# Output projection of the recurrence block with tokens on partitions, last slab by token halves, result scaled and turned by products with a diagonal

## The reference

```python
mix_out = jnp.einsum("bsd,de->bse", merged, w_out[layer])
x = x + rms_norm_2(mix_out, mix_norm_post[layer])
h = rms_norm_2(x, ffn_norm_pre[layer])
up = jnp.einsum("bsd,df->bsf", h, w_up[layer])
up = causal_dwconv(up, conv_f_w[layer], conv_f_b[layer])
gate, val = jnp.split(up, 2, axis=-1)
ffn_out = jnp.einsum("bsf,fd->bsd", jax.nn.gelu(gate) * val, w_down[layer])
x = x + rms_norm_2(ffn_out, ffn_norm_post[layer])
```

## Time and profile before

| | us |
|---|---|
| median of 3 runs | 1138.39 |
| fastest and slowest | 1135.93, 1144.72 |
| the profiled execution | 1130.99 |
| its span, first to last instruction | 1129.2 |
| PE busy in it | 1104.3 (98%) |
| DVE busy | 785.4 (70%) |
| ACT busy | 587.9 (52%) |
| POOL busy | 134.6 (12%) |
| mean granted clock of TensorE, 1 is full | 0.995 |

### The profile page before, as it was taken

The page is one execution under the profiler, slowest core; times in us unless marked ns, Lnnn a source line. Parts: engine busy times, 40 slices in busy tenths (PEclk is TensorE's granted clock), DMA queues, the critical chain, the costliest instruction groups (busy, mean ns, idle before and its releaser), DMA issues.

```text
span 1129.2 us, 21633 instructions
## 1 busy us (share of the span) xinstructions
PE 1104.3 (98%) x9383; PEld 1061.1 (94%) x9383; DVE 785.4 (70%) x1133; ACT 587.9 (52%) x829; POOL 134.6 (12%) x98
## 2 busy tenths in 40 slices
PE   7999899999999999999999999999999989999998
PEld 6988799999999999999999988999988989999998
DVE  6577488784457566977744889795465889888752
ACT  4477655453336555544434476854355647666531
POOL 4200050001230005000122305200000000111000
PEclk9999999999999999999999999999999989999999
DMA  9943056556664444555566473665343645556551
GB/s 281 273 154 112 1 183 191 187 192 201 200 193 151 151 148 149 186 189 187 193 200 198 111 228 96 199 192 188 117 146 113 200 136 187 187 187 206 187 185 40
DMA packets 194866, 192.65 MB, mean 171 GB/s; under 512 B 9691, under 2 KB 192964, under 8 KB 194772
## 3 DMA queue, kind: packets, MB, share of 16 engines
q1 hardware_dynamic: 193680, 190.53, 53.5%
q10 hardware_dynamic: 1092, 0.75, 0.3%
HBM read 189.78 MB, written 1.47 MB: 169 GB/s over the span
## 4 chain that ended last, share of the span: by engine, by line
PE 91%; DVE 4%; ACT 3%; issue 1%; DMA 0%; DVEq 0%; SPq 0%; ACTq 0%
PE ps_gemm L1727 49%; PE ps_trans L1727 33%; PE ps_score L1804 2%; PE ps_out L1842 2%; PE ps_trans L1827 2%; DVE act_lo L1146 1%; DVE xc L1447 1%; DVE w_lo L1140 1%; PE ps_gemm L1914 1%; DMA x_in<-in_x 0%; PE ps_score L1810 0%; PE ps_score L2041 0%; ACT w_hi L756 0%; DVE rs L1152 0%; PE ps_score L1770 0%
## 5 line engine op out<-in xcount | busy, mean ns | idle before, releaser
L1140 DVE TENSOR_TENSOR w_lo<-raw,w_hi 128x2048 fp32r<-128x2048 f32 (+2 forms) x179 | 408.7, 2291 | 44.1 <-ACT w_hi L756 43.7
L756 ACT ACTIVATE w_hi<-raw 128x2048 fp32r<-128x2048 f32 (+2 forms) x179 | 332.4, 1863 | 173.0 <-DMA raw<-in_mlp_w 93.6
L1727 PE MATMUL ps_gemm<-act_hi,w_hi 128*128 128x256 f32 (+1 forms) x960 | 266.2, 285 | 4.8 <-ACT act_hi L1066 4.4
L1727 PE MATMUL ps_gemm<-act_hi,w_lo 128*128 128x256 f32 (+1 forms) x960 | 258.2, 280 | 0.0
L1727 PE MATMUL ps_gemm<-act_lo,w_hi 128*128 128x256 f32 (+1 forms) x960 | 253.9, 280 | 1.2 <-DVE act_lo L1146 1.2
L1727 PE MATMUL ps_trans<-act_hi,w_hi 128*128 128x256 f32 x688 | 191.3, 278 | 1.6 <-DVE w_lo L1140 1.6
L1727 PEld LDWEIGHTS ps_gemm<-act_hi,w_hi 128*128 128x128 f32 (+1 forms) x960 | 181.7, 191 | 10.3 <-issue 8.3
L1727 PE MATMUL ps_trans<-act_lo,w_hi 128*128 128x256 f32 x688 | 191.1, 278 | 0.0
L1727 PE MATMUL ps_trans<-act_hi,w_lo 128*128 128x256 f32 x688 | 191.1, 278 | 0.0
L1727 PEld LDWEIGHTS ps_gemm<-act_hi,w_lo 128*128 128x128 f32 (+1 forms) x960 | 177.7, 188 | 0.3
L1727 PEld LDWEIGHTS ps_gemm<-act_lo,w_hi 128*128 128x128 f32 (+1 forms) x960 | 173.6, 186 | 2.8 <-DVE act_lo L1146 1.6
(11 more groups left out here) (385 smaller groups left out, 2239.6 us busy)
## 6 DMA issues: line engine op xcount, KB each, us to landing
raw<-in_mlp_w SPq DMA_DIRECT2D x64, 1024.0 KB, 5.3
raw<-in_w_in SPq DMA_DIRECT2D x30, 1024.0 KB, 5.3
raw<-in_w_up SPq DMA_DIRECT2D x24, 1024.0 KB, 5.2
raw<-in_od_w_in SPq DMA_DIRECT2D x12, 1024.0 KB, 5.1
raw<-in_w_down SPq DMA_DIRECT2D x12, 1024.0 KB, 5.2
raw<-in_ev_w_in SPq DMA_DIRECT2D x9, 1024.0 KB, 8.1
raw<-in_w_proj_a SPq DMA_DIRECT2D x8, 640.0 KB, 4.2
raw<-in_ev_w_out SPq DMA_DIRECT2D x4, 1024.0 KB, 5.2
```

The source lines that it names most:

```text
L756: act.activation(w_hi[:, slot, 0:k, 0:n], raw[:, slot, 0:k, 0:n], ACT.Copy).then_inc(hi_done, 1)
L1140: dve.tensor_tensor(w_lo[:, slot, 0:k, 0:n], raw[:, slot, 0:k, 0:n], w_hi[:, slot, 0:k, 0:n].bitcast(F32), ALU.subtract).then_inc(w_ready, 1)
L1727: ins = pe.matmul(dst, lhs, rhs, start=(first and opens and opening), stop=(last and closes and i + 1 == len(order)), skip_group_check=True)
```

## The change

The four slabs of `r_out` are multiplied with the tokens standing still in the array (`tok_major=True`), so that the result has tokens on partitions. The last slab is ordered by halves of tokens, each half in a bank of its own (one more group, `EXTRA_GROUPS`), and a semaphore `mix_half_done` tells when the first half is complete. ACT's square gives the sum over features along (`accum_out`), a column of numbers per token half. DVE copies the result into `mix_out` without a gain. For each half a root, a reciprocal of 128x1 and a multiplication of the identity give a diagonal matrix `mix_diag` with the inverse norms. PE multiplies each 128x128 block of `mix_out` by the diagonal, which scales it and turns it back to features on partitions, in `ps_score` and `ps_out`; DVE then forms x = product * gain + x in one instruction per chunk. The sum of squares by the matrix of ones (`stat(5)`) and POOL's two additions are gone, and the norm before the up projection is now number 5. In slab 1 of the up projection its `stat` stands behind chunk 6, no longer chunk 2.

```diff
-EXTRA_GROUPS = {"a_in": 5, "f_dn": 1}
+EXTRA_GROUPS = {"a_in": 5, "r_out": 1, "f_dn": 1}
...
-    mo = ar("mix_out", [P, NX, T], 27 * K)
+    mo = ar("mix_out", [P, TB, D], 27 * K)
+    mdiag = ar("mix_diag", [P, TB, P], 36 * K)
...
+    def mix_bank(gi):
+
+        return (ps_s, ps_o)[gi // 2][:, gi % 2, :]
...
-        pool.wait_ge(sq5, 2)
-        link(pool.tensor_tensor(sq4[:, 0, :, :], sq4[:, 0, :, :], sq4[:, 1, :, :], ALU.add))
-        pool.wait_ge(sq5, 3)
-        pool.tensor_tensor(sq4[:, 0, :, :], sq4[:, 0, :, :], sq4[:, 2, :, :], ALU.add).then_inc(sq_ok, 1)
...
         for j in range(4):
             s = st["r_out"].s0 + j
             split_hi(s + AHEAD)
+            if j == 3:
+                break
             act.wait_ge(slab_done, s + 1)
-            act.activation(sq4[:, j, :, :], result(st["r_out"].g0 + j).rearrange("p (a n) -> p a n", a=2),
-                           ACT.Square).then_inc(sq5, 1)
-        root(5)
+            for tb in range(TB):
+                ins = act.activation(sq4[:, j, tb, :], result(st["r_out"].g0 + j)[:, tb * NS:(tb + 1) * NS], ACT.Square,
+                                     accum_out=mss[:, tb, j:j + 1])
+            ins.then_inc(mix_sq, 1)
+        for tb in range(TB):
+            if tb == 0:
+                act.wait_ge(mix_half, 1)
+            else:
+                act.wait_ge(slab_done, st["r_out"].s0 + 4)
+            act.activation(sq4[:, 3, tb, :], result(st["r_out"].g0 + 3 + tb)[:, tb * NS:(tb + 1) * NS], ACT.Square,
+                           accum_out=mss[:, tb, 3:4]).then_inc(mix_sq, 1)
+            act.wait_ge(mix_sum, 3 + tb)
+            act.activation(rs_m[:, tb:tb + 1], mss[:, tb, 0:1], ACT.Sqrt, scale=1.0 / D, bias=eps_c).then_inc(mix_sd, 1)
...
-        for j in range(4):
-            s, g = st["r_out"].s0 + j, st["r_out"].g0 + j
-            split_lo(s + AHEAD - 1)
-            if j == 3:
-                split_lo(s + AHEAD)
-            dve.wait_ge(sq5, j + 1)
+        s0, g0 = st["r_out"].s0, st["r_out"].g0
+        for j in range(3):
+            split_lo(s0 + j + AHEAD - 1)
+            if j == 2:
+                split_lo(s0 + j + AHEAD)
+            dve.wait_ge(mix_sq, j + 1)
+            if j:
+                dve.tensor_tensor(mss[:, :, 0], mss[:, :, 0], mss[:, :, j], ALU.add).then_inc(mix_sum, 1)
+                dve.wait_ge(mix_sum, j)
+            dve.tensor_copy(mo[:, :, j * NS:(j + 1) * NS], result(g0 + j).rearrange("p (b n) -> p b n", b=TB))\
+                .then_inc(emptied[BANK[g0 + j]], 1)
+        split_lo(s0 + 3 + AHEAD)
+        for tb in range(TB):
+            g = g0 + 3 + tb
+            dve.wait_ge(mix_sq, 4 + tb)
+            dve.tensor_tensor(mss[:, tb, 0:1], mss[:, tb, 0:1], mss[:, tb, 3:4], ALU.add).then_inc(mix_sum, 1)
+            dve.tensor_copy(mo[:, tb, 3 * NS:], result(g)[:, tb * NS:(tb + 1) * NS]).then_inc(emptied[BANK[g]], 1)
+            dve.wait_ge(mix_sd, tb + 1)
+            link(dve.reciprocal(rs_m[:, tb:tb + 1], rs_m[:, tb:tb + 1]))
+            dve.tensor_scalar(mdiag[:, tb, :], ident[:, :], rs_m[:, tb:tb + 1], None, ALU.mult).then_inc(mix_dg, 1)
+        for gi in range(4):
+            dve.wait_ge(mix_x, gi + 1)
             for c in range(2):
-                ins = dve.tensor_scalar(mo[:, 2 * j + c, :], result(g)[:, c * T:(c + 1) * T],
-                                        col("mix_norm_post_2", 2 * j + c), None, ALU.mult)
-            ins.then_inc(emptied[BANK[g]], 1)
-        inv_rms(5)
-        for gi in range(4):
-            c = slice(2 * gi, 2 * gi + 2)
-            link(dve.tensor_tensor(mo[:, c, :], mo[:, c, :], k_pair, ALU.mult))
-            dve.tensor_tensor(x[:, c, :], x[:, c, :], mo[:, c, :], ALU.add).then_inc(x_new, 1)
+                ins = dve.scalar_tensor_tensor(out=x[:, 2 * gi + c, :], in0=mix_bank(gi)[:, c * T:(c + 1) * T],
+                                               scalar=col("mix_norm_post_2", 2 * gi + c), in1=x[:, 2 * gi + c, :],
+                                               op0=ALU.mult, op1=ALU.add)
+            ins.then_inc(x_new, 1)
...
-        out_stage("r_out", m2_hi, m2_lo, before_pair=m2_in)
-        stat(5)
+        s0, g0 = st["r_out"].s0, st["r_out"].g0
+        for j in range(4):
+            gemm(s0 + j, g0 + j, m2_hi, m2_lo, before_pair=m2_in if j == 0 else None, tok_major=True,
+                 second=g0 + 4 if j == 3 else None, by_half=mix_half if j == 3 else None)
+        for tb in range(TB):
+            pe.wait_ge(mix_dg, tb + 1)
+            for gi in range(4):
+                for c in range(2):
+                    k = 2 * gi + c
+                    ins = pe.matmul(mix_bank(gi)[:, c * T + tb * P:c * T + (tb + 1) * P], mo[:, tb, k * P:(k + 1) * P],
+                                    mdiag[:, tb, :], start=True, stop=True)
+                if tb == 1:
+                    ins.then_inc(mix_x, 1)
...
-            gemm(s0 + j, g0 + j, act_hi, act_lo, before_chunk=x_in(6) if j == 0 else None, low_last=j == 0,
-                 between=stat_at(6, 2) if j == 1 else None)
+            gemm(s0 + j, g0 + j, act_hi, act_lo, before_chunk=x_in(5) if j == 0 else None, low_last=j == 0,
+                 between=stat_at(5, 6) if j == 1 else None)
```

More of the change, by code:

```diff
@@ L192, in build @@
     rs_o = place("ffn_rs", [P, TB])
+    mss = place("mix_sums", [P, TB, 4])
+    rs_m = place("mix_rs", [P, TB])
     fw = place("conv_f", [P, 4, 2 * NH2])
@@ L332, in build @@
     half_done = sem("first_half_done")
-    sq5, sq6 = sem("sq5_pairs"), sem("sq6_pairs")
+    sq6 = sem("sq6_pairs")
+    mix_half, mix_sq, mix_sum, mix_sd, mix_dg, mix_x = (sem(n) for n in (
+        "mix_half_done", "mix_sq_ok", "mix_sum", "mix_sd", "mix_diag_ok", "mix_by_feature"))
     x_tok, fsq_ok, fsum, fsd, frs, o_done, o_out = (sem(n) for n in (
@@ L377, in x_ready @@
             return emptied[gi % 2], gi // 2 + 1
-        if n == 6:
+        if n == 5:
             return x_new, gi + 1
@@ L383, in build @@
     PRE = {0: ("norm_mix", 0), 1: ("norm_mlp", 0), 2: ("norm_mix", 8), 3: ("norm_mlp", 8),
-           4: None, 6: ("ffn_norm_pre_2", 0)}
+           4: None, 5: ("ffn_norm_pre_2", 0)}
     PRE_I = {n: i for i, n in enumerate(PRE)}
@@ L1063, in _ @@
         for gi in range(4):
-            act.wait_ge(*x_ready(6, gi))
+            act.wait_ge(*x_ready(5, gi))
             for c in (2 * gi, 2 * gi + 1):
-                act.activation(act_hi[:, c, :], x[:, c, :], ACT.Copy, scale=gain(6, c)).then_inc(xh, 1)
+                act.activation(act_hi[:, c, :], x[:, c, :], ACT.Copy, scale=gain(5, c)).then_inc(xh, 1)
             if gi == 2:
@@ L1071, in _ @@
         square6(3)
-        root(6)
+        root(5)
         s0, g0 = st["f_up"].s0, st["f_up"].g0
@@ L1601, in _ @@
+        for gi in range(4):
+            dve.wait_ge(mix_x, gi + 1)
+            for c in range(2):
+                ins = dve.scalar_tensor_tensor(out=x[:, 2 * gi + c, :], in0=mix_bank(gi)[:, c * T:(c + 1) * T],
+                                               scalar=col("mix_norm_post_2", 2 * gi + c), in1=x[:, 2 * gi + c, :],
+                                               op0=ALU.mult, op1=ALU.add)
+            ins.then_inc(x_new, 1)
         dve.wait_ge(x_new, 4)
-        split_x(6)
+        split_x(5)
@@ L1608, in _ @@
         dve.tensor_tensor(sq4[:, 0, 0, :], sq4[:, 0, 0, :], sq4[:, 0, 1, :], ALU.add).then_inc(sq_ok, 1)
-        inv_rms(6)
+        inv_rms(5)
         dve.wait_ge(zero_pad, 2)
@@ L1750, in stat @@
             pe.wait_ge(sq_ok, n + 1)
[L1751 to L1757, removed]
             if n == 4:
@@ L1762, in stat @@
                 terms = [sq_g[:, 0, 0, :]]
-            elif n == 6:
+            elif n == 5:
                 terms = [sq4[:, 0, 0, :]]
@@ L2098, in _ @@
                 pe.wait_ge(x_new, 4)
-                pe.wait_ge(sd_ok, 7)
+                pe.wait_ge(sd_ok, 6)
                 for tb in range(TB):
```

## The result

| | before | after |
|---|---|---|
| median of the runs, us | 1136.15 | 1173.28 |
| runs; fastest and slowest | 6; 1131.67, 1144.72 | 6; 1172.34, 1175.16 |
| the profiled execution | 1130.99 | 1172.34 |
| its span | 1129.2 | 1170.5 |
| mean granted clock of TensorE | 0.995 | 0.995 |

The changed kernel is slower: after over before is 1.0309, interval 1.0272 to 1.0345. The forecast was 1139.6 with a range to 1144.0; it was wrong, and by far more than any of its terms.

The account below looks back on a forecast made before the run. TensorE was taken as the bound, 91% of the chain, with DVE binding it at up slab 3. -0.4 + 1.6 = +1.2 us on 1130.99 gave 1132.2, carried over to the median as 1139.6, range 1133.5 to 1144.0.

Parts of the forecast that it names:

- the frame of the sum: Everything before the last slab of `r_out` was taken to keep its profiled times, at no cost.
- First diagonal: Between `r_out` and the diagonal products: PE starts these at 912.3, after idling 0.75 us.
- The 32 records of 0.108: Diagonal products, 16 of two records each: 0.108 us per record, 1.73 us per half.
- Slab 0 from the last product of `r_out` on: Up projection's slab 0 starts at 916.2 instead of 917.85, 1.65 us earlier.
- The end of slab 0: Up slab 0 ends at 922.66, before 925.84: TensorE 3.2 us ahead; `stat`, 42 products later, only 0.36 earlier.
- Rival 2: Clock falls already at the hand-over, waiting for the first diagonal: +3.6 us, 1142.0; chance 0.12.
- Slab 3 from that product: Up slab 3 starts only 0.36 us earlier, because the chain from `stat` to its `w_lo` moves only that much.
- That wait: PE, through with up slab 2 at about 934.2, waits some 2.7 us for `w_lo` of slab 3.
- Rival 3: `w_lo` of up slab 3 does not hold PE, so the 3.2 us are kept: 1135.2; chance 0.05.
- The clock: Behind the wait at up slab 3 the clock falls to half, costing 1.6 us.
- Rival 1: Clock stays at 2.4 GHz through the wait at up slab 3: -0.4 us, 1138.0; chance 0.33.
- The sum of the stage up to slab 5: Whole effect of the changed stage: -0.4 + 1.6 = +1.2 us on the profiled execution.

Follow-up runs that it names:

- e1: The kernel before with only 64 unused bytes ahead of `conv_f`, which moves its activations by 64 bytes: 1172.31 us, ratio 1.0331.
- e5: The whole change with its two small tiles in the arena, so no old tile moves, against the kernel before: 1137.08 us, ratio 1.0007.
- e2: The changed kernel with another 64 unused bytes ahead of `conv_f`, activations 128 bytes from where the kernel before has them: 1149.8 us, ratio 1.012 to before.
- e8: The kernel before with 256 unused bytes ahead of `conv_f`: 1137.62 us in one run.
- e11: e5 with `stat` back behind chunk 2 of up slab 1, where the kernel before has it: 1130.56 us, ratio 0.9975 to before.
- e12: The kernel before, unchanged, run once more for a second trace: 1134.43 us in one run.

## Why the prediction was wrong

**The step that failed** is the frame of the sum, in the words "what is before the last slab stays where it is", and with it the pace of 0.1175 us per product, carried over from before to the changed kernel. (It is itself an average: its 96 products go at 0.113 up to 937 us and at 0.118 behind.) Nothing in the text costs the two tiles' placement, so it stood at nothing without a reason. What the runs showed in its place is 0.120 through the whole program. Of the 41.3 us that the span grew by, 34.96 came ahead of the last product of `r_out`, where the program's products are the same. e1 has them with 64 bytes and nothing else; e5 has the whole change without them. No rival held this either, and the range rested on the same cases. The chance of 0.95 for no change was a chance over the mechanisms I had listed, all of which lay in one stage.

**The steps of the stage,** read in the changed kernel and in e5, were near:

- First diagonal: idle time of PE 0.75 by the forecast, measured 0.22 after, 0.33 in e5. The way from the end of `w_lo` (945.81) to that record is 0.97, where the forecast had 1.2.
- The 32 records of 0.108: the 16 of the first half take 1.89 (946.78 to 948.67), forecast 1.73. Behind the first few they stand 0.112 apart. Near.
- Slab 0 from the last product of `r_out` on: forecast 1.65 less than before, measured 1.93 less (4.60, which is 950.88 less 946.28, against 6.53, 917.85 less 911.32) and 1.83 less in e5. Near.
- The end of slab 0: forecast 3.2 us ahead of before, counted from the last product of `r_out`. Measured by the start of the 42 products ahead of `stat`: 11.08 (957.36 less 946.28) against 14.52, so 3.44 ahead. Then `stat`: forecast 0.36 ahead, measured 16.12 (962.40 less 946.28) against 16.64, so 0.52, and 0.83 in e5. Right: the gain is spent on the 24 more products.
- Clock in slab 0: forecast full, the window 950.90 to 957.20 has 1.00. Rival 2 falls: the hand-over did not cost the clock.
- Slab 3 from that product: forecast 0.36 less than before's 25.85, measured 25.33 and 25.02. The direction and the cause are right: the 3.2 us turn into a wait.
- That wait: forecast 2.7 us, measured 2.31 after and 2.64 in e5, in both by `w_lo` of slab 3. Rival 3, that `w_lo` wouldn't hold PE, falls.
- The clock: forecast a fall worth 1.6. The window behind the wait has PEclk 0.58 after, and in e5 two slabs take 12.53 where 96 products at full pace take 10.88, 1.65 lost. Rival 1 falls. The Trainium skill (TensorE: Matmul & The Clock Gate, "Why this matters for your kernels") advises against gaps of over about 3 us between bursts; by it a gap of this length would not cost the clock. Here it did, behind 2.31 and 2.64 us and behind the 2.43 of e2 (PEclk 0.50 from 953.20 to 956.50), so the measurement decides. The rival was right in one thing, that more than the length counts: a wait of 1.97 us that ends at 662.36 in the changed kernel left the clock full (1.00 from 650 to 664), and one of 1.87 that ends at 644.52 in e8 was followed by 0.50 from 646.10 to 649.40.
- The sum of the stage up to slab 5: forecast +1.2, measured +1.16 after and +0.12 in e5. That after meets it is luck in part: its products are 2.2 ns slower there than before's and e5's are 4.5 ns faster, about 0.2 to 0.4 us for two slabs. One trace of each doesn't tell where between the two the stage's cost lies.

In e5 the old tiles stay where they were, which the forecast took for granted. It lies at 1.0007 of before, inside the 1% that the forecast counted as no change; that leaves its +1.2 us neither confirmed nor refuted by the times. The wait that the forecast named is also where the change's own gain went: e11 moves `stat` back and gets the 3.7 us in the trace.

**What stays open.** Why the operands' distance matters: the next product's weights are loaded from SBUF while the current one's columns are read from it (`PEld` is busy 94% of the span beside PE's 98%), and a collision of the two readings would fit. One stretch of the changed kernel speaks for it. Where the standing operand has 16 columns and not 128, so that its load shows as 0.09 us and not 0.19, the products stand 0.113 apart at difference 0 too, with 0.120 on either side:

```profile
679.84 0.28 PE L1756 MATMUL ps_gemm<-act_lo,w_hi 128*16 128x256 f32 x1
...
682.33 0.28 PE L1756 MATMUL ps_gemm<-act_hi,w_lo 128*16 128x256 f32 x1
```

These are 22 products in 2.49 us. No run here shows the collision itself. What picks one of the two paces at a given difference: it holds through long streams and changes mostly at a late product or where the kind of operand that stands changes; e8 excludes that the place modulo 256 alone picks it, and more isn't known. Differences finer than 32 bytes, and other shapes, weren't tried.

## What to carry to other kernels

Compare first a stretch that the edit doesn't touch: if the same 96 products take another time there at the same granted clock, the edited stage is the wrong place to look for that loss. Take several such stretches, since one kernel went at two paces from one execution to the next. A new tile placed ahead of the operands of products is an edit to every product behind it; keep the byte places of the old tiles, and try some paddings between the weights' and the activations' tiles as a change of its own, since here 64 bytes alone moved the kernel by 3.3%. And when a step is freed, ask what else hung on the step moved along with it: `stat` behind 24 more products gave back what the new hand-over had won.

## What the runs showed of the hardware

- The pace of products of 128x128 by 256 columns in the rounded format (fp32r) depended on the byte place of the moving operand less that of the standing one, modulo 128: 120.0 ns at 0, 116.7 (in parts 117.8) at 32, 113.3 or 117.8 at 64, 118.3 at 96, all at a granted clock of 1.00. It held with the weights standing and with the tokens standing. With 16 standing columns it was 113.3 at 0 too.
- At the difference 64 two paces occur, each held for long (113.3 for nearly all these products from 449 to 768 us in e12), in the same program and from one execution to the next; in e11 the step from 113.3 to 117.8 fell on a product that came 0.05 us late. At 0 one occurs, and the runs scatter less: 1172.16 to 1175.16 over ten runs of two kernels, against 1128.01 to 1146.44 for before.
- The granted clock fell to half at waits of 2.31 us (after), 2.43 (e2) and 2.64 (e5) between dense streams of products, and behind one of 1.87 in e8, where one of 1.97 in the changed kernel left it full. It stayed full through a hand-over of 4.6 us that was filled with 32 small records.
- A plain float32 product of 128x128 by 128 columns costs two records of 0.11 us at full clock (0.112 in the changed kernel).
